# An earlier, half-tile opening and wider splits of the inputs of w_out and w_down in one transformer layer on one core

## The reference, cut to what matters

```
xn = rmsnorm(x, norm_mix_g);  p = split(xn @ w_in)        # w_in: 2048 x 16424
y_fox = forgetting attention;  y_gdn = gated DeltaNet;  y_ml = mLSTM   (8 heads each)
y = g0*(y_fox @ w_fox_proj) + g1*(y_gdn @ w_gdn_proj) + g2*(y_ml @ w_ml_proj)
x = x + y @ w_out                                          # w_out: 2048 x 2048
h = causal conv(rmsnorm(x, norm_ffn_g) @ w_up);  u, gt = h # w_up: 2048 x 11264
x = x + (silu(gt) * u) @ w_down                            # w_down: 5632 x 2048
out = rmsnorm(x, norm_final_g)
```

## Time and profile before

| | us |
|---|---|
| median of 3 runs | 1897.83 |
| lowest, highest | 1894.27, 1905.62 |
| profiled execution, its own time | 1906.58 |
| its span, first to last instruction | 1904.8 |
| TensorE busy (98%) | 1860.1 |
| VectorE busy (56%) | 1069.0 |
| ScalarE busy (44%) | 847.6 |
| GpSimd busy (24%) | 453.2 |
| mean granted TensorE clock, share of full | 0.989 |

### The profile page before, as it was taken

One profiled execution on the slowest core, in us unless ns is written; L12 is line 12 of the kernel. 1 busy time (PEld: TensorE's weight loads), 2 busy tenths in 40 slices (PEclk: granted clock), 3 DMA queues, 4 the chain that ended last, 5 costly groups with the idle time before them and its releaser, 6 DMA issues.

```text
span 1904.8 us, 27440 instructions
## 1 busy us (share of the span) xinstructions
PE 1860.1 (98%) x10317; PEld 1593.4 (84%) x10317; DVE 1069.0 (56%) x1315; ACT 847.6 (44%) x1030; POOL 453.2 (24%) x241
## 2 busy tenths in 40 slices
PE   6999999999999999999999999999999999999997
PEld 5888899888877888888888778888888888888886
DVE  4766754355565675555555447666666666533334
ACT  5445443433553354444444454444444444444444
POOL 4212353212122122222222232222222222222223
PEclk9999999999999999999999999999999999999999
DMA  6555543444543456666667545665666656655553
GB/s 179 160 160 169 153 133 111 117 127 144 157 142 111 133 166 192 191 186 182 191 193 244 189 157 172 187 188 178 188 185 185 189 182 189 210 185 181 191 188 128
DMA packets 263139, 324.44 MB, mean 170 GB/s; under 512 B 16746, under 2 KB 230180, under 8 KB 262180
## 3 DMA queue, kind: packets, MB, share of 16 engines
q1 hardware_dynamic: 263076, 323.58, 55.7%
HBM read 321.44 MB, written 2.10 MB: 170 GB/s over the span
## 4 chain that ended last, share of the span: by engine, by line
PE 92%; DVE 3%; ACT 1%; issue 1%; POOL 1%; SPq 1%; DMA 0%; DVEq 0%; ACTq 0%; POOLq 0%
PE ps L518 91%; ACT w_hi L354 1%; DVE w_lo L359 1%; DVE xs L1665 0%; DVE acc L1493 0%; DMA raw<-in_w_in_dram 0%; PE ps L776 0%; SPq L446 0%; PE ps L607 0%; POOL nlv L1782 0%; DVE xnT L1208 0%; SPq L449 0%; PE ps L582 0%; DVE x L1648 0%; DVE dmax L1350 0%
## 5 line engine op out<-in xcount | busy, mean ns | idle before, releaser
L518 PE MATMUL ps<-xnT,w_hi 128*128 128x512 f32 (+1 forms) x2960 | 1055.8, 400 | 11.1 <-DVE xnT L1208 6.3
L354 ACT ACTIVATE w_hi<-raw 128x1024 fp32r<-128x1024 f32 (+1 forms) x601 | 632.8, 1058 | 862.8 <-PE ps L518 845.5
L359 DVE TENSOR_TENSOR w_lo<-raw,w_hi 128x1024 fp32r<-128x1024 f32 (+1 forms) x451 | 565.4, 1260 | 532.6 <-ACT w_hi L354 532.0
L518 PE MATMUL ps<-xnT,w_lo 128*128 128x256 f32 (+1 forms) x2960 | 834.0, 282 | 0.0
L359 POOL TENSOR_TENSOR w_lo<-raw,w_hi 128x1024 fp32r<-128x1024 f32 x150 | 366.5, 2444 | 1368.8 <-ACT w_hi L354 1368.7
L518 PEld LDWEIGHTS ps<-xnT,w_hi 128*128 128x128 f32 (+1 forms) x2960 | 558.4, 189 | 148.0 <-issue 7.7
L518 PEld LDWEIGHTS ps<-xnT,w_lo 128*128 128x128 f32 (+1 forms) x2960 | 561.8, 190 | 0.3
L518 PE MATMUL ps<-w_hi,side 128*128 128x512 f32 x960 | 303.8, 397 | 0.0
L518 PEld LDWEIGHTS ps<-w_hi,side 128*128 128x128 f32 x960 | 180.8, 188 | 45.4 <-DVE side L1605 0.7
L518 PE MATMUL ps<-w_lo,side 128*128 128x512 f32 x480 | 190.3, 396 | 0.0
L518 PE MATMUL ps<-w_hi,xnT 128*128 128x512 f32 x512 | 171.0, 401 | 1.9 <-DVE w_lo L359 1.9
(11 more groups left out here) (320 smaller groups left out, 1269.5 us busy)
## 6 DMA issues: line engine op xcount, KB each, us to landing
raw<-in_w_in_dram SPq DMA_DIRECT2D x256, 512.0 KB, 3.8
raw<-in_w_up_dram SPq DMA_DIRECT2D x176, 512.0 KB, 3.8
raw<-in_w_down_dram SPq DMA_DIRECT2D x88, 512.0 KB, 4.3
raw<-in_w_out_dram SPq DMA_DIRECT2D x32, 512.0 KB, 4.1
raw<-in_w_fox_proj_dram SPq DMA_DIRECT2D x16, 512.0 KB, 3.4
raw<-in_w_gdn_proj_dram SPq DMA_DIRECT2D x16, 512.0 KB, 3.3
raw<-in_w_ml_proj_dram SPq DMA_DIRECT2D x16, 512.0 KB, 3.5
x_in<-in_x_dram SPq DMA_DIRECT2D x2, 1024.0 KB, 5.9
```

The lines of the kernel that those rows point to most:

```text
L354: act.activation(w_hi[:, s, 0:n], raw[:, s, 0:n], ACT.Copy).then_inc(hi_ready[s], 1)
L359: eng.tensor_tensor(w_lo[:, s, 0:n], raw[:, s, 0:n], w_hi[:, s, 0:n], ALU.subtract).then_inc(lo_ready[s], 1)
L518: return pe.matmul(o, l, r, start=start, stop=stop)
```

## The change

1. The first unit is now gdn 0 and the small unit the second (chunk 4). x is loaded in four half tiles (128 x 1024), behind one load of the norm's gain as a row; the first four weight chunks follow, then the parameter rows, the biases and, behind the low half of chunk 0, the small unit's three loads.
2. TensorE spreads the gain over 128 partitions into PSUM (four matmuls of `ones` by `g_row`), VectorE scales each half tile by the reciprocal root and the gain into `xg`, TensorE transposes eight blocks at a time, and ScalarE and VectorE split eight k tiles of one token tile in one instruction each. Chunk 0 starts when the first eight k tiles of both token tiles are split; the last eight transposes come behind chunk 0. The parameter rows are transposed behind chunk 2. GpSimd builds the level masks behind its splits of chunks 1 and 3.
3. In w_out the first two k tiles still go through `side`, in one copy and one subtraction. The other fourteen go to their own place in `xnT`, in pieces of 4, 4, 4 and 2 k tiles, copied right behind the gates. In w_down the first two k tiles go through `side`, the others two at a time through a ring of three pairs in `xnT`; a round of the loop is twelve chunks.

Cut to its core:

```diff
-UNITS = [("small", 0, 0)]
-UNITS += [("gdn", GDN_QKV + 256 * g, g) for g in range(12)]
+UNITS = [("gdn", GDN_QKV, 0), ("small", 0, 0)]
+UNITS += [("gdn", GDN_QKV + 256 * g, g) for g in range(1, 12)]
...
+SMALL = 4
...
+MIXED = ((2, 6), (6, 10), (10, 14), (14, 16))
+RING = 3
+DOWN_ROUNDS = (FKT // 2 - 1) // RING
...
+        xg = part("xg", 4, [P, NT, D])
+        g_row = part("g_row", 2, [1, D])
...
+            def load_x(tt):
+
+                for half in range(2):
+                    cols_ = slice(CHUNK * half, CHUNK * half + CHUNK)
+                    sp.dma_start(x_in[:, tt, cols_], xf[:, tt, cols_]).then_inc(x_loaded[2 * tt + half], 16)
+
...
+            def load_first(c):
...
+                if c == SMALL:
+                    s = c % SLOTS
+                    sp.wait_ge(lo_ready[s], c // SLOTS)
+                    r0 = raw[:, s, 0:640].rearrange("p (t n) -> p t n", n=40)
+                    for at, n, dst in ((FOX_F, 8, 0), (GDN_B, 16, 8), (ML_I, 16, 24)):
+                        sp.dma_start(r0[:, :, dst:dst + n], w[:, :, at:at + n]).then_inc(raw_loaded[s], 16)
...
+            load_x(0)
+            load_x(1)
+            for c in range(SLOTS):
+                load_first(c)
...
+            def row_chunk(c, it, x, first, tiles=(0, 1), free=None):
+
+                s, half = c % SLOTS, (c - N2) % 2
...
+            def turn_first(n):
...
+                pe.wait_ge(S["xs_ready"], (1, 3, 3, 4)[n])
+                if n == 3:
+                    pe.wait_ge(xt_first[0], 1)
+                for t in range(8):
+                    kt = 8 * half + t
+                    last = pe.transpose(ps[:, first_bank(tt, half) + t // 4, (t % 4) * P:(t % 4) * P + P],
+                                        xg[:, tt, kt * P:kt * P + P], ident[:, :])
+                last.then_inc(S["xt_written"], 1)
+
...
+                if c == 0:
+                    turn_first(3)
...
+                    pe.wait_ge(S["side_ready"], (j + 4) // 8 + 1)
+                if j < 4:
+                    row_chunk(N2 + j, 0, side[:, j // 2, :], j < 2, (1, 0),
+                              (pair_read[1], 2 * (GROUPS // 2) + 1) if j == 0 else None)
+                else:
+                    row_chunk(N2 + j, 0, xnT[:, j // 2, :], False)
...
+            def ring_round(i, n):
+                for j in range(n):
+                    if j % 4 == 0:
+                        pe.wait_ge(S["side_ready"], i * RING + (7 + j // 4))
+                    row_chunk(N4 + 4 + j, i * RING, xnT[:, j // 2, :], False)
...
+            def first_sums(tt, half):
+
+                act.wait_ge(x_loaded[2 * tt + half], 16)
+                chain(f(x_sq[:, 0:CHUNK], x_in[:, tt, CHUNK * half:CHUNK * half + CHUNK], ACT.Square,
+                        accum_out=ss[:, 0, 2 * tt + half:2 * tt + half + 1]))
+                if half == 0:
+                    chain(f(start_b[:, tt:tt + 1], ss[:, 0, 2 * tt:2 * tt + 1], ACT.Identity, scale=1.0 / D, bias=eps_c[:, 0:1]))
+                else:
+                    f(rstd[:, 0, tt:tt + 1], ss[:, 0, 2 * tt + 1:2 * tt + 2], ACT.Sqrt, scale=1.0 / D,
+                      bias=start_b[:, tt:tt + 1]).then_inc(S["sums_ready"], 1)
...
+            def first_hi(n):
+
+                act.wait_ge(S["xt_written"], n + 1)
+                hi, _, src = turned_first(*FIRST[n])
+                f(hi, src, ACT.Copy).then_inc(S["xt_hi"], 1)
...
+            first_hi(0)
             split_hi(act, 0)
-            act.wait_ge(S["cols_ready"], 1)
-            turn_x_hi()
+            first_hi(1)
+            split_hi(act, 1)
+            first_hi(2)
+            split_hi(act, 2)
+            split_hi(act, 3)
+            first_hi(3)
...
+                            chunk_done(act, N2 - 3)
+                            act.wait_ge(S["y_ready"], GROUPS + 24)
+                            mixed_hi(0)
...
+            mixed_hi(1)
+            mixed_hi(2)
+            act.wait_ge(S["y_ready"], GROUPS + 32)
+            mixed_hi(3)
...
-                    if j % 2:
-                        side_hi(N4 + j, i, hT[:, bass.ds(i * 2 + (2 + j // 2), 1), :].rearrange("p a b -> p (a b)"), j // 2)
+            with act.Fori(0, DOWN_ROUNDS) as i:
+                for j in range(4 * RING):
+                    split_hi(act, N4 + SLOTS + j, i * RING)
+                    if j % 4 == 0:
+                        b = j // 4
+                        chunk_done(act, N4 + j - 1, i * RING)
+                        if b == 0:
+                            act.wait_ge(S["h_ready"], FF // 256)
+                        f(xnT[:, 2 * b:2 * b + 2, 0:SEQ], hT[:, bass.ds(i * (2 * RING) + (2 + 2 * b), 2), :],
+                          ACT.Copy).then_inc(S["side_hi"], 1)
...
+            def first_scale(tt, half):
+
+                if half == 0:
+                    dve.wait_ge(S["sums_ready"], tt + 1)
+                    chain(dve.reciprocal(rstd[:, 0, tt:tt + 1], rstd[:, 0, tt:tt + 1]))
+                dve.wait_ge(S["g_spread"], 2 * half + 2)
+                at = slice(CHUNK * half, CHUNK * half + CHUNK)
+                dve.scalar_tensor_tensor(xg[:, tt, at], x_in[:, tt, at], rstd[:, 0, tt:tt + 1],
+                                         ps[:, 6 - 4 * half:8 - 4 * half, :].rearrange("p b n -> p (b n)"),
+                                         ALU.mult, ALU.mult).then_inc(S["xs_ready"], 1)
+
+            def first_lo(n):
+
+                dve.wait_ge(S["xt_hi"], n + 1)
+                hi, lo, src = turned_first(*FIRST[n])
+                tt_(lo, src, hi, ALU.subtract).then_inc(xt_first[FIRST[n][0]], 1)
...
+            first_scale(0, 0)
+            first_scale(0, 1)
+            first_scale(1, 0)
+            first_lo(0)
             split_lo(dve, 0)
-            turn_x_lo()
+            first_lo(1)
+            first_scale(1, 1)
+            first_lo(2)
+            split_lo(dve, 2)
+            first_lo(3)
...
+            def side_lo(n, x, src):
+
+                dve.wait_ge(S["side_hi"], n)
+                tt_(x[:, :, SEQ:2 * SEQ], src, x[:, :, 0:SEQ], ALU.subtract).then_inc(S["side_ready"], 1)
+
+            def mixed_lo(n):
+
+                a, b = MIXED[n]
+                side_lo(n + 2, xnT[:, a:b, :], yT[:, a:b, :])
...
+            for n in range(4):
+                mixed_lo(n)
...
+                        split_lo(dve, N4 + SLOTS + j, i * RING)
+                    if j % 4 == 1:
+                        b = j // 4
+                        side_lo(i * RING + (7 + b), xnT[:, 2 * b:2 * b + 2, :],
+                                hT[:, bass.ds(i * (2 * RING) + (2 + 2 * b), 2), :])
...
+            chain(pool.memset(tiny[:, 1, :], 0.0))
+            pool.memset(tiny[:, 1, :], 0.0).then_inc(S["consts"], 1)
+            split_lo(pool, 1)
+            split_lo(pool, SLOTS - 1)
```

More of the change, by code:

```diff
@@ L58 @@
 N1 = len(CHUNKS)
+SMALL = 4
+assert UNITS[CHUNKS[SMALL][0]][0] == "small"
 def last_chunk(kind, g):
@@ L227, in hybrid_layer_kernel @@
         norm_b = small("norm_b", [P, 2, NT])
+        start_b = small("start_b", [P, NT])
         arena = cursor[0] + (-cursor[0]) % 32
@@ L335, in hybrid_layer_kernel @@
         S = {n: sem(n) for n in names}
-        x_loaded = [sem(f"x_loaded{tt}") for tt in range(NT)]
+        x_loaded = [sem(f"x_loaded{n}") for n in range(2 * NT)]
+        xt_first = [sem(f"xt_first{tt}") for tt in range(NT)]
         pair_read = [sem(f"pair_read{p}") for p in range(2)]
@@ L546, in tokens @@
                 last.then_inc(chunk_used[s], 1)
-            def row_chunk(c, it, first, tiles=(0, 1), free=None):
-                s, k2, half = c % SLOTS, (c - N2) // 2 % 2, (c - N2) % 2
+            def row_chunk(c, it, x, first, tiles=(0, 1), free=None):
+                s, half = c % SLOTS, (c - N2) % 2
                 pe.wait_ge(lo_ready[s], c // SLOTS + 1 + it)
@@ L555, in row_chunk, with last_rows @@
                     for q in range(2):
-                        last = three(ps[:, 4 * tt + 2 * half + q, :], side[:, k2, :], tt, s,
+                        last = three(ps[:, 4 * tt + 2 * half + q, :], x, tt, s,
                                      512 * q, 512 * q + 512, first, False)
                 last.then_inc(chunk_used[s], 1)
-            def last_rows(c0, n):
+            def last_rows(c0, x2, n):
                 order = [(0, k2, half) for k2 in range(2) for half in range(2)]
@@ L567, in last_rows @@
                     if tt == 0:
-                        if half == 0:
-                            pe.wait_ge(S["side_ready"], n - 1 + k2)
+                        pe.wait_ge(S["side_ready"], n)
                         pe.wait_ge(lo_ready[s], c // SLOTS + 1)
                     for q in range(2):
-                        last = three(ps[:, 4 * tt + 2 * half + q, :], side[:, k2, :], tt, s,
+                        last = three(ps[:, 4 * tt + 2 * half + q, :], x2[:, k2, :], tt, s,
                                      512 * q, 512 * q + 512, False, k2 == 1)
@@ L777, in item, with turn_rows @@
                 last.then_inc(item_done[k % 2], 1)
```

(31 more changed lines are left out.)

217 lines of the change are left out of this document (80 added, 137 removed).

## The result

| | before | after |
|---|---|---|
| median of 20 runs, us | 1898.28 | 1891.73 |
| lowest, highest | 1894.27, 1909.43 | 1881.64, 1898.73 |
| mean of the 20 | 1900.90 | 1889.95 |
| profiled execution, its own time | 1906.58 | 1893.68 |
| its span | 1904.8 | 1891.9 |

The ratio is 0.9935, with a 95% interval of 0.9918 to 0.9952: 0.65% less, 9 to 16 us. The times of either kernel lie in two groups about 10 us apart (before 1894 to 1901 and 1905 to 1909, after 1882 to 1885 and 1891 to 1899), and the two medians fell in different ones, so the medians differ by only 6.6 while the means differ by 11.0 and the profiled executions by 12.9. The forecast was 1891 from a gain of 7.0.

A forecast was written before the change was run, and what follows sets the result against it. TensorE's stream was taken as the bound. Opening 7.4 less 0.4 for small waits, w_out 0 and w_down 0 gave 7.0 off the 1897.83 median: 1891 us, own range 1886 to 1896, 8-in-10 range 1884 to 1899.

The forecast's parts named there:

- What bounds the kernel: Whole kernel: a stream on TensorE, where only a hole or a half clock costs time; w_out and w_down have neither.
- Part 1, the opening: Opening: chunk 5 begins at 35.6 instead of 43.0, a gain of 7.4 us, 7.0 after small waits.
- x: Opening, loading and squaring x: first square at about 4.5, second root at about 11.0 (before 10.7), so scaled no earlier.
- The gain row: Opening, four matmuls of ones by g_row: 1.7 us, 3.5 at half clock; taken as nothing, between 0 and 0.5.
- First matmul: Opening, start of chunk 0 after scaling, transposes and splits: 16.6 us, with ends 15.4 and 17.5.
- From there: Opening, chunk 0 to chunk 5: chunks of 2.8 us, chunk 5 at 35.6; moved loads, masks and softplus cost nothing.
- 0.4 off for small waits: Opening: 0.4 us taken from the 7.4 gain for the features and the hand-overs at chunks 1 and 3.
- Rival B: Opening: chunk 0 and the eight transposes behind it run at half clock, 3.1 us lost, gain 3.9, time 1894; chance 0.13.
- Part 2, w_out: w_out: fewer, wider splits bring 0; fifth chunk's low half hidden with 1.0 us to spare; ends 0 and 2 lost.
- Part 3, w_down: w_down: the ring's pair is ready with 2.6 us to spare, 21 times; matmuls unchanged in number and shape; gain 0.
- rival E: w_down ring: chain to the subtraction takes 6.4 us instead of 3.0, TensorE waits 21 times; slower, 1908; chance 0.04.
- Rival C: Opening and behind: x 1.1 us sooner, full clock 0.6, a half-clock stretch gone 1.6; gain 10.3, time 1887.5; chance 0.16.

## Why the prediction was right, and where not

**What bounds the kernel: right, and its conclusion too narrow.** TensorE's stream does bound it. "Only a hole in it or a half clock costs time" was wrong: the distance between two matmuls at full clock is not a constant. Three rates of the same 128x512 matmul with a stationary activation were measured at four offsets, from the counts in 200 us of w_down: 0.2339 us with the operand at 480, 0.2320 at 512, 0.2262 at 128 and at 1152.

**Part 1, the opening: right in kind, 7.0 was about 5.6.** Over all profiled executions the piece of 852 starts at 248.9 on the mean with the old opening (six, 246.3 to 250.1) and 243.4 with the new (seven without the features' edit, 241.5 to 246.5), a gain of 5.5. By its terms:
- *x.* The first half landed at 5.47 instead of 4.5, as late as a whole tile had the earlier trace rows; perhaps because with halves and the weight chunks behind them more was under way at once, which no run tests. The second root ended at 11.49 instead of 11.0, as four squares and their followers took 6.0, not 6.3.
- *The gain row.* Taken as nothing, and nothing it was, but by luck. The bound was wrong: the four products took 7.16 us, not 1.7 to 3.5. They show as eight instructions, two for each, at 0.89 a piece: one instruction costs what the sum had at half clock for a whole product (3.5 / 4), which it had priced by transposes. They ended at 9.93; the first transposes were ready to go at 10.10.
- *First matmul* at 17.45, forecast 16.6, inside the ends of 15.4 and 17.5.
- *From there* no wait at all up to chunk 5, which began at 35.97 for 35.6. The small loads and the moved softplus stayed hidden, as said; the level masks not quite, as the next point shows.
- *The failed term* is the "0.4 off for small waits (the features, hand-overs at chunk 1 and 3)". The features alone cost 1.6 (0.8 to 2.1 in the seven executions with the new opening and this order). The reduction to `feat` stood behind VectorE's split, which took 2.59 instead of 1.23 beside GpSimd's and ended 1.09 after it (39.92 and 38.83). GpSimd's split in turn stood behind the level masks, which ended at 36.35. The prediction had those at nothing because TensorE wants GpSimd's split only at 41.5; it did not ask what runs beside it. Taking the features first removed the wait.
- *The start of the count.* Chunk 5 of before began at 43.21 in the profiled execution, of which 20 to 45 had a mean clock of 0.86, and at 41.6 to 41.9 in the five others with the old opening (0.93 to 1.00). Over all profiled executions the new opening brings chunk 5 forward by 5.6, not 7.2.
- *The clock behind it.* From 80 to 105 the mean clock was 0.80 to 0.93 in the six executions with the old opening (mean 0.84) and 0.86 or 0.93 in the eight with the new one (mean 0.90). That is about 1.5 of the average gain of 5.5; in the profiled pair both had 0.86.

**Rival B, half clock in the opening: false here, and true in one execution of eight.** The second pair of chunk 0 was already at full pace (17.87 to 18.21: 0.34 a pair, where 0.63 was a pair at half). Nearly all of the 24 transposes ahead of it ran at half pace (16 in 3.41 us, 0.21 each, where eight behind chunk 0 took 1.04 in all and the spacing to the next matmul was 0.79). So the full pace came up with nothing on TensorE but the gain's products and transposes. It does not always: with the small buffers at 480, chunk 0 began like this.
```profile
18.68 0.63 PE L560 MATMUL ps<-xnT,w_hi 128*128 128x512 f32 x1
...
19.33 0.63 PE L560 MATMUL ps<-xnT,w_hi 128*128 128x512 f32 x1
```
That is 0.65 a pair, and 4.55 us to the transposes behind chunk 0 instead of 2.85: 1.7 lost. The other seven with the new opening were at full pace by the second pair, behind the same instructions, and why this one was not is open. The clock column reads 1.00 in both, from chunk 0 to chunk 1, so half and full are read from the pace here. The Trainium skill, "TensorE: Matmul & The Clock Gate", "Part 4: PE-mode transpose", has it that transposes don't engage the full clock. These traces do not agree: in the kernel before, the pace of the transposes doubled with nothing else on TensorE, and here eight ran at full pace behind chunk 0. Ahead of chunk 0 the gain's products may have had their share; no run tells the two apart.

**Part 2, w_out: no stall, right; 0 wrong.** VectorE's four subtractions ended at 1053.41 and nobody waited. But w_out was 2.8 shorter.

**Part 3, w_down: no stall, right, so rival E fell; 0 wrong, and this is the step that failed.** "TensorE's matmuls are the same in number and shape, with xnT for side. I take 0; nothing above 0 can be had where the engine never idles." With xnT for side was the change that mattered: from 480 to 128 modulo 2048, 0.2339 to 0.2262 us a matmul, times some 1056, 8 us. Moving side alone by 1696 bytes gives the same, the wider splits without the place do not. The prediction's own sign of being wrong, a total that falls by more than the opening gives, came true.

**A term that nobody had.** Part 1 adds `start_b`, 32 bytes ahead of every small buffer. It costs 3.2 us in the stretch ahead of w_out, and gives 0.7 back where side is still used for all of w_out.

**The sum.** The two profiled executions differ by 5.6 by 250 us, 2.8 in w_out and 8.0 in w_down, less 3.2 ahead of w_out, less 0.3 in the small remainders of the balance: 12.9. The prediction had 7.0 + 0 + 0. That it met the median at 1891.7 is luck: the medians of the two kernels fell in different groups, before in its lower and after in its upper. By the ratio the gain is 0.65%, some 12 us, just above the 0.5% within which I had put the result with 0.72. Rival C (1887.5, more than the sum) had the right direction, in the main for the wrong reason: x did not land sooner. Its half-clock stretch that falls away (1.6) is borne out on the average (1.5), though not in this pair.

## What to carry to other kernels

"Always busy" on TensorE does not mean that nothing is to be gained or lost: count the matmuls per microsecond in a long stretch at full clock and compare it among stages that do the same work (here w_out, w_down, w_up). When a change moves a buffer, or adds a small one ahead of others, the byte offset of everything behind it is part of the change; try the offset by itself, since it is one line (here 0.9886 of the time of before, against 0.9935 for the whole change without it; 5.7 us of that are in the traces). Count a gain from more than one profile where the stage varies: chunk 5 of before began at 43.2 in the one that I had, and at 41.6 to 41.9 in five others. And where a new unit is put between others, follow what its first reader stands behind on its engine.

## What the hardware showed that I had not expected

**The place of the stationary operand.** At full clock, in a stretch without any wait, the same matmul with its stationary operand at another byte offset starts every 0.2339 (480), 0.2320 (512) or 0.2262 us (128, 1152). Over all fourteen profiled executions w_down took 247.9 to 248.0 us at 480 (two), 245.8 to 246.0 at 512 (two), and 239.8 to 240.4 at 128 or 1152 (ten), whatever the opening, the width of the splits and the pace of w_up. Why is open; the weights it multiplies lie at 128 modulo 2048 in all these kernels, so it may be the distance to them that counts, and no run moved those.

**Moving other buffers changes the pace of matmuls that don't read them.** One gate chunk group ahead of w_out is 64 matmuls over xnT and w_hi or w_lo, none of which any run moved. Its first matmul and the one behind its last, with the small buffers at 480:
```profile
793.80 0.40 PE L560 MATMUL ps<-xnT,w_hi 128*128 128x512 f32 x1
...
804.90 0.40 PE L560 MATMUL ps<-y_ml,w_hi 128*128 128x512 f32 x1
```
And in the changed kernel, at 512:
```profile
791.89 0.39 PE L560 MATMUL ps<-xnT,w_hi 128*128 128x512 f32 x1
...
803.18 0.39 PE L560 MATMUL ps<-y_ml,w_hi 128*128 128x512 f32 x1
```
11.10 against 11.29 us for the same work, without a wait in either; there are 20 such groups ahead of w_out in the piece of 2352, so 3.8 us, of which the groups of y's products between them, somewhat quicker at 512, give back the 0.6 that is over 3.2. At 128 the same group takes 11.10 again, and a group of y's products, whose moving operand does lie in the moved block, 5.54 against 5.64 at 480 and 5.62 at 512. What the accesses of which engine meet there is open.

**Two paces of w_up.** In w_up, with no wait and at full clock, this is a stretch of the kernel with small buffers at 128:
```profile
1200.00:1600.00 400.00, 400.00 (x2267) 346.91 (x2266) 259.57 (x373) 182.28 (x177) 83.88 (x35) 1.00 0.60 185
```
And the same stretch with the features first, an edit that ends before 45 us:
```profile
1200.00:1600.00 400.00, 400.00 (x2310) 352.69 (x2309) 264.00 (x380) 184.84 (x180) 86.77 (x36) 1.00 0.63 189
```
2267 against 2310 matmuls in 400 us is 1.9%, some 9 us over w_up (498.1 to 499.6 in ten executions, 488.7 to 489.7 in four), about the distance between the two groups of times. Of the profiled executions four had the quick pace (1877.2, 1881.7, 1888.5 and 1891.3 us, each in its kernel's lower group). All others had the slow one. All four have the new opening, but so do four of the slow ones. It looks drawn at each execution, but no kernel was profiled in both, so that is argued and not shown.

**The price of an f32 product of one row.** The gain's product (one partition by 512 columns, f32) took 7.16 / 4 = 1.79 us at the low pace of the opening, in two instructions, where a split matmul of 512 columns at full clock started every 0.23. How much of that is the type, the pace or the one row, no run shows.

**A split beside a split.** VectorE's 1.23 us subtraction took 1.77 to 2.60 where it started while GpSimd's was running, and ended 1.07 to 1.09 us after GpSimd's in all seven such cases at this chunk (39.92 after 38.83, and 39.15 after 38.08, by the lines above). So by its end times it made next to no headway until GpSimd's was done: the later GpSimd starts, the later VectorE ends.
